# Four experts in fixed order instead of three, and blocks of 96, 80 and 64 columns in the expert stage

## The reference, cut to what matters

```
expert, gate = hier_route(xf, lp)      # group by top 1, then 2 of its 8 experts, per token
xs[dest] = xf[tok_sorted]              # tokens sorted by expert
ys = (silu(xb @ w1[e]) * (xb @ w3[e])) @ w2[e]
out.at[tok_sorted].add(ys[dest] * g_sorted)
```

## Time and profile before

| | |
|---|---|
| median of three runs | 1432.16 us |
| profiled execution | 1430.49 us |
| its span, first to last instruction | 1428.7 us |
| TensorE busy | 1284.4 us (90%) |
| VectorE, ScalarE, GpSimd busy | 426.9, 333.7, 229.9 us |
| mean granted TensorE clock | 0.954 |
| DMA | 273.74 MB, mean 192 GB/s |
| first matmul of the expert stage (gather transposes) | at 837.4 us |

### The profile page before, as it was taken

How to read it: one execution, slowest core, us unless ns; L and a number is a source line. 1 busy time by engine, 2 the same in 40 slices (tenths; PEclk the granted TensorE clock), 3 DMA queues, 4 the chain that set the end, 5 groups by cost and what they waited for, 6 DMA issues and landing times.

```text
span 1428.7 us, 37955 instructions
## 1 busy us (share of the span) xinstructions
PE 1284.4 (90%) x16430; PEld 968.5 (68%) x16430; DVE 426.9 (30%) x873; ACT 333.7 (23%) x775; POOL 229.9 (16%) x318
## 2 busy tenths in 40 slices
PE   5899999955899999999999859999898989988995
PEld 2444444423666567666567559999898988988985
DVE  2210001036555446445444651111111111111110
ACT  4310010023544445454454200000001001000010
POOL 3100000003221222122120111111112111111101
PEclk9999999976989999999999979999999999999998
DMA  8012111050120122012030946999999999999992
GB/s 304 15 43 86 43 43 71 28 209 26 51 75 16 60 76 76 16 61 70 4 123 21 416 148 238 362 371 373 362 376 375 386 378 381 381 378 376 381 391 76
DMA packets 39709, 273.74 MB, mean 192 GB/s; under 512 B 9208, under 2 KB 13176, under 8 KB 27340
## 3 DMA queue, kind: packets, MB, share of 16 engines
q1 hardware_dynamic: 32944, 253.78, 45.9%
q0 software_dynamic: 6400, 17.84, 5.2%
q10 hardware_dynamic: 288, 1.05, 0.2%
HBM read 246.32 MB, written 30.48 MB: 194 GB/s over the span
## 4 chain that ended last, share of the span: by engine, by line
PE 69%; DMA 14%; issue 7%; DVE 4%; ACT 3%; POOL 2%; SPq 1%; POOLq 0%; ACTq 0%; DVEq 0%
PE psum L795 17%; PE psum L1058 16%; DMA arena<-in_w 12%; PE psum L1084 9%; PE psum L910 7%; PE psum L949 4%; PE psum L981 3%; PE psum L961 2%; PE psum L749 2%; PE psum L855 2%; PE psum L1094 1%; PE psum L764 1%; PE psum L1049 1%; POOL small L1461 1%; PE psum L896 1%
## 5 line engine op out<-in xcount | busy, mean ns | idle before, releaser
L1058 PE MATMUL psum<-arena 128*64 128x80 f32 (+1 forms) x8192 | 330.3, 243 | 31.3 <-DMA arena<-in_w 28.0
L1058 PEld LDWEIGHTS psum<-arena 128*64 128x64 f32 x8192 | 319.6, 142 | 41.6 <-issue 37.3
L795 PE MATMUL psum<-arena 128*128 128x512 f32 (+1 forms) x576 | 238.1, 574 | 0.6 <-DVE arena L1672 0.6
L795 PEld LDWEIGHTS psum<-arena 128*128 128x128 f32 x576 | 108.8, 190 | 124.2 <-issue 124.2
L1084 PE MATMUL psum<-arena 128*64 128x80 f32 (+1 forms) x4096 | 158.8, 239 | 5.3 <-issue 5.3
L1084 PEld LDWEIGHTS psum<-arena 128*64 128x64 f32 x4096 | 155.0, 139 | 6.1 <-issue 6.1
L910 PE MATMUL psum<-arena 128*128 128x512 f32 x288 | 127.0, 594 | 1.7 <-DVE arena L1912 1.0
L1418 ACT ACTIVATE arena<-psum,slot_gate 96x1024 f32<-96x1024 f32 x32 | 35.5, 1111 | 354.6 <-PE psum L1094 354.6
L749 PE MATMUL psum<-ident,arena 128*128 128x128 f32 (+1 forms) x432 | 65.2, 286 | 46.9 <-DVE arena L1766 18.2
L910 PEld LDWEIGHTS psum<-arena 128*128 128x128 f32 x288 | 53.3, 190 | 63.0 <-issue 61.4
L749 PEld LDWEIGHTS psum<-ident,arena 128*128 128x128 f32 (+1 forms) x432 | 50.8, 139 | 64.4 <-DVE arena L1653 19.8
(11 more groups left out here) (233 smaller groups left out, 1280.2 us busy)
## 6 DMA issues: line engine op xcount, KB each, us to landing
arena<-in_w SPq DMA_DIRECT2D x96, 2048.0 KB, 17.3
arena<-in_x_rows SPq DMA_DIRECT2D x18, 512.0 KB, 5.5
z_rows<-arena SPq DMA_DIRECT2D x9, 980.0 KB, 4.5
arena<-in_w_in SPq DMA_DIRECT2D x1, 7840.0 KB, 23.4
arena<-z_rows SPq DMA_DIRECT2D x9, 768.0 KB, 5.8
arena<-in_w_out SPq DMA_DIRECT2D x1, 4096.0 KB, 17.1
out_y<-arena SPq DMA_DIRECT2D x8, 512.0 KB, 2.6
xn_rows<-arena SPq DMA_DIRECT2D x8, 512.0 KB, 3.0
```

Source lines behind the costliest of these rows:

```text
L795: ins = pe.matmul(o[:, 0:hi - lo], xT[s][:, k, :], w_in[:, k, lo:hi], start=(k == 0), stop=(k == KD - 1))
L1058: ins = pe.matmul(o[c:c + CT, j * EB:j * EB + rows], w[:, k, j * P + c:j * P + c + CT], x[:, k, 0:rows], start=(k == 0), stop=(k == KD - 1))
```

## The change

It makes `FIRST` 4, so that experts 0 to 3 are the first four. Place 3 uses set 0 and no longer waits for `order_ok`; its w1 waits for one count of `h1_full` (place 0 done), where it waited for two. Sets 1 and 2 take turns from place 4 on: place 4 waits for the blocks of place 1 where it waited for those of place 2; place 5 waits for place 2 where it waited for 3; from place 6 on the waits are those of before (for place p-2).

The widths are now 96 columns for places 0 to 10, 80 for 11 to 24 and 64 for 25 to 31 in the up blocks (`down` of a place runs with the width of the next one). The scatter's lists are 96 long for places 0 to 9, 80 for 10 to 23 and 64 for 24 to 31. The gather always takes a list of 96. On TensorE places 1 to 4 are written out, then come three loops of two experts per body: 5 to 10, 11 to 24, 25 to 30. `list_overflow` has three more small instructions; at most 28 extra blocks are provided for, where it was 26.

```diff
-EL = 80
-FIRST = 3
-BIG = 8
+FIRST = 4
+BLOCKS = ((0, EB), (10, 80), (24, 64))
-MAX_OVER = 2 * TOKENS // (EL + 1)
+MAX_OVER = 28
...
         def set_of(p):
-            return 0 if p == 0 else 1 + (p - 1) % SETS
-        def load_next(eng, p, s):
-            e = eng.value_load(order_e[0:1, bass.ds(p, 1)], min_val=0, max_val=NE - 1)
-            row, free = ahead(eng, e * P), ahead(eng, p - (SETS - 1))
+            return p % 3 if p < FIRST else 1 + p % 2
+        def load_next(eng, p, s, free):
+            if isinstance(p, int) and p < FIRST:
+                row = p * P
+            else:
+                row = ahead(eng, eng.value_load(order_e[0:1, bass.ds(p, 1)], ...) * P)
+            free = ahead(eng, free)
             eng.wait_ge(h1_full, free)
...
+            load_next(sp_, 3, set_of(3), 1)
             sp_.wait_ge(order_ok, 1)
-            with sp_.Fori(0, rounds) as j:
-                for i in range(SETS):
-                    load_next(sp_, SETS * j + FIRST + i, set_of(FIRST + i))
+            for p in range(FIRST, FIRST + 2):
+                load_next(sp_, p, set_of(p), p - 2)
+            with sp_.Fori(0, (NE - FIRST - 2) // 2) as j:
+                for i in range(2):
+                    p = 2 * j + FIRST + 2 + i
+                    load_next(sp_, p, set_of(FIRST + i), p - 1)
...
-            for p in range(1, FIRST):
+            for p in range(1, FIRST + 1):
                 expert(p, EB)
-            with pe.Fori(0, (BIG + 1 - FIRST) // 2) as j:
-                for i in range(2):
-                    expert(FIRST + i, EB, j)
-            with pe.Fori(0, (NE - 2 - BIG) // 2) as j:
-                for i in range(2):
-                    expert(BIG + 1 + i, EL, j)
-            expert(NE - 1, EL)
+            starts = [FIRST] + [lo for lo, _ in BLOCKS[1:]] + [NE - 2]
+            for (_, rows), lo, hi in zip(BLOCKS, starts, starts[1:]):
+                with pe.Fori(0, (hi - lo) // 2) as j:
+                    for i in range(2):
+                        expert(lo + 1 + i, rows, j)
+            expert(NE - 1, rows)
...
-            def gather(s, b, e, signal, rows):
+            def gather(s, b, e, signal):
...
-                fetch(s, rows, now_tok[s][0:rows], signal)
+                fetch(s, EB, now_tok[s][0:EB], signal)
...
-                link(TS(R["cap"], R["pos"], float(BIG), float(EL - EB), ALU.is_ge, ALU.mult))
-                link(TS(R["cap"], R["cap"], float(EB), None, ALU.add))
+                link(dve.memset(R["cap"], float(EB)))
+                for (_, before_), (lo, rows) in zip(BLOCKS, BLOCKS[1:]):
+                    link(TS(R["key"], R["pos"], float(lo), float(rows - before_), ALU.is_ge, ALU.mult))
+                    link(TT(R["cap"], R["cap"], R["key"], ALU.add))
```

More of the change, by code:

```diff
@@ L354, in build @@
             "goh": (NT, NG), "ge": (NT, NG), "cnt": (NE,), "key": (NE,), "pos": (NE,), "cap": (NE,), "ov": (NE,),
-            "ovend": (NE,), "base": (NE,), "order": (NE,), "cols": (20, NT), "over": (MAX_OVER + 1,),
+            "ovend": (NE,), "base": (NE,), "cols": (20, NT), "over": (MAX_OVER + 1,),
             "tabs": (2 * NT, 2 * NE), "rows": (2 * NT, P)}.items()}
@@ L551, in set_of, with loads_of @@
         def set_of(p):
-            return 0 if p == 0 else 1 + (p - 1) % SETS
-        def load_next(eng, p, s):
-            e = eng.value_load(order_e[0:1, bass.ds(p, 1)], min_val=0, max_val=NE - 1)
-            row, free = ahead(eng, e * P), ahead(eng, p - (SETS - 1))
+            return p % 3 if p < FIRST else 1 + p % 2
+        def loads_of(p):
+            return 16 * (1 + p // 3 if p < FIRST else 2 + (p - FIRST) // 2)
+        def load_next(eng, p, s, free):
+            if isinstance(p, int) and p < FIRST:
+                row = p * P
+            else:
+                row = ahead(eng, eng.value_load(order_e[0:1, bass.ds(p, 1)], min_val=0, max_val=NE - 1) * P)
+            free = ahead(eng, free)
             eng.wait_ge(h1_full, free)
@@ L705, in _ @@
             sp_.wait_ge(m_store, 32)
+            load_next(sp_, 3, set_of(3), 1)
             sp_.wait_ge(order_ok, 1)
-            rounds = (NE - FIRST) // SETS
-            with sp_.Fori(0, rounds) as j:
-                for i in range(SETS):
-                    load_next(sp_, SETS * j + FIRST + i, set_of(FIRST + i))
-            for p in range(FIRST + SETS * rounds, NE):
-                load_next(sp_, p, set_of(p))
+            for p in range(FIRST, FIRST + 2):
[4 more added lines that the diff above has]
+                    load_next(sp_, p, set_of(FIRST + i), p - 1)
             sp_.wait_ge(yT_full, NE)
@@ L1099, in expert @@
                 b = p if j is None else p + 2 * j
-                loaded = lambda q: (16 if q == 0 else 16 * ((q - 1) // SETS + 1)) + (0 if j is None else 16 * j)
-                fetched = lambda q: 16 * (q // 2 + 1) + (0 if j is None else 16 * j)
+                more = 0 if j is None else 16 * j
                 w, s, old = set_of(p), p % 2, set_of(p - 1)
-                hidden_1(w, s, b, w1_in[w], loaded(p), rows)
-                down(old, b - 1, w2_in[old], loaded(p - 1), rows)
+                hidden_1(w, s, b, w1_in[w], loads_of(p) + more, rows)
+                down(old, b - 1, w2_in[old], loads_of(p - 1) + more, rows)
                 if p < NE - 1:
-                    gather_transposes(1 - s, b + 1, xe_in[1 - s], fetched(p + 1))
-                hidden_3(w, s, b, w3_in[w], loaded(p), rows)
+                    gather_transposes(1 - s, b + 1, xe_in[1 - s], 16 * ((p + 1) // 2 + 1) + more)
+                hidden_3(w, s, b, w3_in[w], loads_of(p) + more, rows)
                 turn_back(b - 1)
@@ L1113, in _ @@
             hidden_3(0, 0, 0, w3_in[0], 16, EB)
-            for p in range(1, FIRST):
+            for p in range(1, FIRST + 1):
                 expert(p, EB)
-            with pe.Fori(0, (BIG + 1 - FIRST) // 2) as j:
-                for i in range(2):
-                    expert(FIRST + i, EB, j)
-            with pe.Fori(0, (NE - 2 - BIG) // 2) as j:
-                for i in range(2):
-                    expert(BIG + 1 + i, EL, j)
-            expert(NE - 1, EL)
-            last = set_of(NE - 1)
-            down(last, NE - 1, w2_in[last], 16 * ((NE - 2) // SETS + 1), EL)
+            starts = [FIRST] + [lo for lo, _ in BLOCKS[1:]] + [NE - 2]
[3 more added lines that the diff above has]
+                        expert(lo + 1 + i, rows, j)
+            last, rows = set_of(NE - 1), BLOCKS[-1][1]
+            expert(NE - 1, rows)
+            down(last, NE - 1, w2_in[last], loads_of(NE - 1), rows)
             turn_back(NE - 1)
@@ L1584, in scatter @@
                                         oob_is_err=False).then_inc(signal, 16)
[L1586 to L1594, removed]
             for s in range(2):
@@ L1598, in _ @@
                 fetch(s, EB, slot_out[0:EB, s:s + 1], xe_in[s])
-            pool.wait_ge(xeT_full, 1)
-            fetch(0, EB, slot_out[0:EB, 2:3], xe_in[0])
+            for s in range(2):
+                pool.wait_ge(xeT_full, s + 1)
+                fetch(s, EB, slot_out[0:EB, s + 2:s + 3], xe_in[s])
             pool.wait_ge(order_ok, 1)
[L1602 to L1605, removed]
+            ends = [lo for lo, _ in BLOCKS[1:]] + [NE - 4]
+            for (lo, rows), hi in zip(BLOCKS, ends):
                 with pool.Fori(lo // 2, hi // 2) as j:
@@ L1608, in _ @@
                         b = 2 * j + s
-                        e = turn(b, s, j, more)
+                        e = column(b + 4)
+                        pool.wait_ge(xeT_full, b + 3)
+                        pool.sem_inc(index_steps, 1)
+                        gather(s, b + 4, e, xe_in[s])
+                        e = column(b)
                         scatter(s, b, e, ye_out[s], ye_out[1 - s], 16 * (j + s), rows)
             for b in range(NE - 4, NE):
-                e = turn(b, b % 2, b // 2, 0)
-                scatter(b % 2, b, e, ye_out[b % 2], ye_out[1 - b % 2], 16 * (b // 2 + b % 2), EL)
+                e = column(b)
+                scatter(b % 2, b, e, ye_out[b % 2], ye_out[1 - b % 2], 16 * (b // 2 + b % 2), BLOCKS[-1][1])
             pool.wait_ge(over_ok, 1)
@@ L1622, in _ @@
                         pool.sem_inc(index_steps, 1)
-                        gather(0, NE + j, NE + j, ov_xe, EB)
+                        gather(0, NE + j, NE + j, ov_xe)
                         scatter(0, NE + j, NE + j, ov_ye, ov_ye, 16 * j, EB)
@@ L2011, in list_order @@
                 link(TT(sort[0:1], sort[0:1], bc1(iota[0:1, 0:NE], square), ALU.mult))
-                link(dve.tensor_reduce(R["order"][0:1], sort[0:1], AX, ALU.add))
-                dve.tensor_copy(order_e[:], R["order"][0:1]).then_inc(order_ok, 1)
+                link(dve.tensor_reduce(R["base"][0:1], sort[0:1], AX, ALU.add))
+                dve.tensor_copy(order_e[:], R["base"][0:1]).then_inc(order_ok, 1)
             def floor_blocks(dst, src, add):
```

## The result

The changed kernel takes 1464.67 us (median of four runs, 1461.06 to 1475.6) against 1432.38 for the kernel before in the same comparison: ratio 1.0237, 95% interval 1.0176 to 1.0299. It is 2.4% slower. The forecast was 1430.8 with a range of 1423 to 1440, so it was wrong, and on the wrong side.

The account below looks back on a forecast made before the run. The weight stream, plus TensorE's work after the last w1, was taken to set the end. -3.1 + 3.5 - 1.8 = -1.4 us on 1430.49 gave 1429.1, plus 1.67 for the median: 1430.8 us, range 1423 to 1440.

Parts of the forecast that it names:

- A third pair of fresh loop code: First pass of the 64-column loop, places 25 and 26: 6.9 to 12 us of TensorE's time, slack 10, counted 0.
- P: Follow-up theory: code comes in 256-instruction pieces; a loop touching 8, not 7, can refetch at jumps back, gaps 11 to 12 us.
- C: Rival, places 5 to 12: gaps of fresh code delay the weight stream, +11 us, 1443 us; chance 10%.
- the earlier load: Place 3's weights go out 12 to 18 us earlier; net -3.1 us at the end, bounds -5.0 and +2.5.
- the stream: Weight loads setting the end: longer gather lists and changed scatter lists add +3.5 us, bounds -1.3 and +5.5.
- the tail: Work behind the last w1: narrower blocks and shorter last scatter, less a clock cost, net -1.8 us, bounds -3.7 and +1.0.
- What bounds it: Mid-stage, the weight stream at 18.2 us per expert sets the end, plus TensorE's work after the last w1.
- The gather lists: Fullest DMA engine carries list length divided by 16; places 8 to 31 gather one row more, 24 x 0.20 = +4.8 us.
- The widths: Four 64-column blocks behind the last w1 save 3.4 us; with clock cost and shorter last scatter, net -1.8 us.
- The +1.9 us for the clock: Slower block after some 3 us of TensorE idling ahead of `hidden_1` of 31: +1.9 us, between 0 and 2.6.

Follow-up runs that it names:

- the kernel moved by 90: Changed kernel plus 90 idle instructions in TensorE's stream while it waits for the first gather, against the kernel before: 1434.33 us, ratio 0.9992.
- the run with two sets: Changed kernel plus 90 idle instructions, weight sets and waits as before (earlier load of place 3 undone), against the kernel before: 1437.31 us, ratio 1.0029.

## Why the prediction was wrong, step by step

**The step that failed** is "A third pair of fresh loop code". It put it thus: "By the page every pass of the loops would fetch; by the rows only the first does", and counted 0 us. The rows were right, for that kernel. The earlier trace rows show a loop that was not fetched again because it lay well, 75 instructions ahead of a piece's end with 7 in its eighth piece. I took the trait of one placement for a trait of loops. The rule of the Trainium skill that I weighed there ("Runtime: NRT & Kernel Launch", Instruction fetch mechanics: a taken branch whose target has left the window stalls until it is fetched) is what happened, but not with the window of two blocks that I took from it: a body of 7 pieces went round without a fetch. The same section gives TensorE room for 2048 instructions, which is eight pieces, and I did not weigh that. It fits P; no run measured the store. The step also priced only TensorE's gaps in a first pass, 6.9 to 12 us with 10 of slack. The third loop's first pass did no harm that shows: in the kernel moved by 90 its longest gap was 2.8 us, and a wait of 7.1 us for weights came behind it. What cost 29 us were 46 us of gaps at jumps back of the second loop, whose body was nearly the same as before but stood elsewhere.

None of the rivals had it either. C was the nearest: gaps of fresh code that reach the stream, at places 5 to 12, 1443 us. It had the kind of wait and the direction, but neither the place nor the price.

**The rest, against the kernel moved by 90**, which is the change without that effect. The forecast for it was 1.4 us less than before; measured is 0.1% less [0.4% less, 0.2% more]. That the two agree is in part luck. In the two profiled executions the parts below make 0 us for the earlier load, +7.1 for the stream and -2.5 for the tail, +4.6 us in all (spans 1433.3 and 1428.7), where -3.1, +3.5 and -1.8 were forecast. Ten executions of the kernel moved by 90 spread over 10.4 us, so no single trace settles a part of this size.

- *What bounds it*: right. DMA share 0.99 and 34.5 us of waits for weights.
- *The earlier load*: w1 of place 3 went out at 846.8 us as forecast, w2 of place 6 waited for `down` of place 4. In the changed kernel it was issued at 938.4 us and landed after 9.2, where it had been 12.5; moved by 90, at 941.2 and 9.1:

```profile
L549 SPq DMA_DIRECT2D arena<-in_w x1: 332/332/332, 941.2 to 941.2; - x1
DMA to landing us min/median/max: 9.1/9.1/9.1
```

  It landed at 950.3, exactly when it did before: the shorter queue was used up by 3.4 us that TensorE came later. The net of -3.1 was too good in this trace; the run with two sets leaves 0 to -8.
- *The gather lists*: right in mechanism. The gathers alone were priced at 24 x 0.20 = 4.8 us; shorter lists save 4.4 and 4.8 us in the two pairs of runs. The sum with the scatters came out too low: the period went from 18.19 to 18.48 where +3.5 us makes 18.33, or 7.1 us over the stretch, beyond the bound of +5.5. No run separates the scatters.
- *The widths*: a block at 64 columns takes 3.9 us (3.8 forecast), and the last w1 is followed by 33.3 us to the end of the span (34 forecast, 35.8 before). The +1.9 us for the clock was not paid: the step assumed that TensorE would idle some 3 us ahead of `hidden_1` of 31. A wait of 4.39 us ahead of `hidden_1` of 30 was followed by a block at 6.17, but TensorE was then busy right up to the last block of w1, which took 3.95 (the timeline of TensorE in the kernel moved by 90):

```profile
1384.35 6.17 PE L1068 MATMUL psum<-arena 128*64 128x64 f32 x128 [4.39 <-DMA arena<-in_w]
...
1398.88 1.08 PE L1104 MATMUL psum<-ident,arena 128*96 128x128 f32 x8
1400.04 3.95 PE L1068 MATMUL psum<-arena 128*64 128x64 f32 x128
```

  The rule of the Trainium skill ("TensorE: Matmul & The Clock Gate", LDWEIGHTS), taken as a serial limit, would make such a block 6.8 us. The trace does not show that limit: 128 pairs took 3.95 us.

## What to carry to other kernels

Where an engine runs a long loop body, look up where its code lies before and after a change: count the packets of the instruction queue in a stretch in which the loop goes round, and look for "issue" gaps at its jumps back and for jump instructions that last microseconds. If they are there, a few idle instructions ahead of the loop can settle it (eight did here), and until that is done no other part of the change can be judged. A loop that shows no such gaps is no evidence for the next kernel, in which every instruction ahead of it counts.

## What the runs showed of the hardware

- TensorE's code is fetched in pieces of 256 instructions (16.3 KB a packet, gaps 256 instructions apart in a first pass). In these traces no loop of 1618 that touched 7 pieces shows such gaps at its jumps back; one that touched 8 with 57 to 79 instructions in the last did so at 4 of 6, 2 of 2 and 8 of 10 jumps back, each time 9 packets and about 10 to 12 us, of which the jump instruction itself lasted 6.7 to 7.9 us, against 0.2.
- Why it is not every jump back, and why a loop with 7 instructions in an eighth piece (the kernel before) does not suffer, is open. A store of eight pieces that reads one ahead fits both the 9 packets and the second; no run measured the store itself.
- The length of an indirect DMA's list costs time even where its entries name no row. The same rows in lists of 80 instead of 96 were 4.4 us cheaper over 24 gathers (between the medians of two comparisons), and in lists of 96, 80 and 64 by place 4.8 us cheaper (1433.03 and 1428.21, in one comparison).
- An idle wait costs TensorE's queue about 0.11 us (165 of them filled 826.5 to 844.4 us).
